# A sparse attention stage: its eight query blocks in a new order, top-k picks taken earlier, banded logits in mid-slot

## What is computed

```python
def swa_sink_attention(q, k, v, sinks, rel_table):   # banded: 8 heads, window 128
    ...
def block(args):                                     # sparse: once per 128 queries (block n)
    ql, iqb, iwb, n = args
    t = n * QB + jnp.arange(QB)
    dots = jnp.einsum('bqhd,bsd->bqhs', iqb, ik) * (IDX_DIM ** -0.5)
    score = jnp.einsum('bqh,bqhs->bqs', iwb, jax.nn.relu(dots))
    score = jnp.where(causal[None], score, NEG_INF)
    _, idx = lax.top_k(score, topk)                  # topk = 256
    ...
    logits = jnp.einsum('bqhc,bqkc->bhqk', ql, sel)  # plus bias of the distance
    p = jax.nn.softmax(logits, axis=-1)
    o_lat = jnp.einsum('bhqk,bqkc->bqhc', p, sel)
```

## Time and profile before

| what | us |
|---|---|
| median of 3 runs | 3803.22 |
| lowest and highest | 3801.25, 3818.11 |
| profiled execution, its own time | 3799.82 |
| its span | 3798.0 |
| TensorE, VectorE, ScalarE, GpSimd busy | 3341.8, 1476.6, 872.9, 745.3 |
| mean granted TensorE clock | 0.928 of full speed |

### The profile page before, as it was taken

One profiled execution on the slowest core, in us unless ns is written; L12 is line 12 of the kernel. 1 busy time (PEld: TensorE's weight loads), 2 busy tenths in 40 slices (PEclk: granted clock), 3 DMA queues, 4 the chain that ended last, 5 costly groups with the idle time before them and its releaser, 6 DMA issues.

```text
span 3798.0 us, 37215 instructions
## 1 busy us (share of the span) xinstructions
PE 3341.8 (88%) x14990; PEld 2463.6 (65%) x14990; DVE 1476.6 (39%) x2594; ACT 872.9 (23%) x1530; POOL 745.3 (20%) x322
## 2 busy tenths in 40 slices
PE   5996888887789878999999977999997589999998
PEld 2443344444677777788888854446877578888886
DVE  3013688998342135322222242302463722222225
ACT  2113333433312212111111122101341122112111
POOL 2000000000321103323323320001111433223223
PEclk9995788888889989999999988999998789999999
DMA  5100111111112101111111131010002202111112
GB/s 143 42 23 22 49 52 45 45 45 23 56 56 95 34 18 43 47 55 44 45 55 44 52 120 53 22 47 0 26 1 97 92 23 56 50 50 44 55 45 111
DMA packets 173178, 192.24 MB, mean 51 GB/s; under 512 B 24268, under 2 KB 137804, under 8 KB 172285
## 3 DMA queue, kind: packets, MB, share of 16 engines
q1 hardware_dynamic: 163696, 177.20, 14.8%
q10 hardware_dynamic: 9356, 13.31, 1.1%
HBM read 174.71 MB, written 15.78 MB: 50 GB/s over the span
## 4 chain that ended last, share of the span: by engine, by line
PE 60%; issue 16%; DVE 13%; POOL 6%; ACT 3%; DMA 1%; ACTq 1%; POOLq 0%; SPq 0%; DVEq 0%
PE psum L606 9%; PE psum L608 9%; PE psum L607 9%; PE psum L599 7%; PE psum L589 6%; POOL weights_parts L2150 3%; PE psum L971 3%; PE psum L709 2%; DVE x_cols L1596 2%; DVE rows L1594 2%; PE psum L703 2%; POOL region L2198 2%; DVE stats L1514 1%; PE psum L747 1%; PE psum L728 1%
## 5 line engine op out<-in xcount | busy, mean ns | idle before, releaser
L2150 POOL TENSOR_TENSOR weights_parts<-weights,weights_parts 128x2048 fp32r<-128x2048 f32 (+1 forms) x82 | 377.0, 4597 | 982.9 <-ACT weights_parts L1093 982.9
L606 PE MATMUL psum<-x_cols_parts,weights_parts 128*128 128x512 f32 x1344 | 525.0, 391 | 25.3 <-POOL weights_parts L2150 23.6
L608 PE MATMUL psum<-x_cols_parts,weights_parts 128*128 128x512 f32 x1344 | 524.3, 390 | 0.0
L608 PE MATMUL psum<-weights_parts,region_parts 128*128 128x512 f32 (+1 forms) x1120 | 410.0, 366 | 0.0
L606 PE MATMUL psum<-weights_parts,region_parts 128*128 128x512 f32 x864 | 337.2, 390 | 6.7 <-DVE region_parts L2104 5.8
L607 PE MATMUL psum<-weights_parts,region_parts 128*128 128x512 f32 x864 | 336.9, 390 | 0.0
L606 PEld LDWEIGHTS psum<-x_cols_parts,weights_parts 128*128 128x128 f32 x1344 | 253.4, 189 | 79.1 <-issue 24.6
L608 PEld LDWEIGHTS psum<-x_cols_parts,weights_parts 128*128 128x128 f32 x1344 | 253.2, 188 | 52.7
L607 PE MATMUL psum<-x_rows_parts,weights_parts 128*128 128x512 f32 x704 | 274.6, 390 | 0.0
L1093 ACT ACTIVATE weights_parts<-weights 128x2048 fp32r<-128x2048 f32 (+1 forms) x82 | 155.0, 1890 | 468.7 <-DMA region<-in_bup_h_dram 142.4
L606 PE MATMUL psum<-weights_parts,x_cols_parts 128*128 128x256 f32 x768 | 222.2, 289 | 27.8 <-POOL wide_parts L2176 11.7
(11 more groups left out here) (285 smaller groups left out, 5185.8 us busy)
## 6 DMA issues: line engine op xcount, KB each, us to landing
weights<-in_ada_w_dram SPq DMA_DIRECT2D x24, 1024.0 KB, 5.2
weights<-in_ffn_up_w_dram SPq DMA_DIRECT2D x44, 512.0 KB, 4.8
weights<-in_w_up_dram SPq DMA_DIRECT2D x16, 1024.0 KB, 5.1
weights<-in_w_down_dram SPq DMA_DIRECT2D x16, 1024.0 KB, 5.1
weights<-in_m_in_w_dram SPq DMA_DIRECT2D x7, 2048.0 KB, 9.1
weights<-in_ffn_down_w_dram SPq DMA_DIRECT2D x10, 1024.0 KB, 5.1
weights<-in_xa_wkv_dram SPq DMA_DIRECT2D x4, 2048.0 KB, 8.0
x_rows<-x_scratch SPq DMA_DIRECT2D x4, 2048.0 KB, 11.3
```

The lines of the kernel that those rows point to most:

```text
L606: pe.matmul(o, lhsT=a_hi, rhs=b_hi, start=(first and i == 0), stop=False)
L608: m = pe.matmul(o, lhsT=a_lo, rhs=b_hi, start=False, stop=(last and i == len(terms) - 1))
L2150: pool.tensor_tensor(WLO[buf][:, 0:width], WRAW[buf][:, 0:width], WHI[buf][:, 0:width], ALU.subtract).then_inc(s("w_lo"), 1)
```

## The change

- `ORDER = (1, 7, 6, 5, 4, 3, 2, 0)`: step n works on block `ORDER[n]`, and every width, slice and condition follows the block instead of the step. Steps 0 and 7 (blocks 1 and 0) need no pick.
- The picks of step 1 (block 7, 1024 columns) are spread over the 15 slots from (-1, 0) to (0, 6): two rounds in each of 13, three in the last two. The picks of later steps stay where they were relative to the step: four rounds in slot 7 of step m - 2, 28 in step m - 1.
- The index dots, Relu and sums of block 7 are done ahead of the loop, in PSUM banks 0 to 3, with two new semaphores, `ix0_l` and `ix0_e`; VectorE waits for `attn_in` behind them.
- VectorE's order in a slot: bias add, maximum, `index_sum`, `window_max`, the first half of the rounds, `window_scores`, reciprocal, second half, `window_sum`.
- The modulation pieces stay where they were: four in each of steps 1 to 6.

```diff
+ORDER = (1, 7, 6, 5, 4, 3, 2, 0)
+FIRST_ROUNDS = (2,) * 13 + (3, 3)
...
+def picking(n):
+
+    return 0 <= n < NT and ORDER[n] >= 2
+
+
+def pick_rounds(n, i):
+
+    g = NH * n + i + NH
+    if g < len(FIRST_ROUNDS):
+        a = sum(FIRST_ROUNDS[:g])
+        return 1, a, a + (FIRST_ROUNDS[g] + 1) // 2, a + FIRST_ROUNDS[g]
+    m, r = (n + 2, 0) if i == NH - 1 else (n + 1, 4 * i + 4)
+    return (m, r, r + 2, r + 4) if picking(m) else None
...
-    if k >= 2 and k < NT:
+    if k >= 2 and picking(k):
         jobs["ix0"] = ("ix", k, h, 0)
-        if (k + 1) * P > BW:
+        if (ORDER[k] + 1) * P > BW:
             jobs["ix1"] = ("ix", k, h, 1)
...
             pe.wait_ge(f_free, FT["memT"])
+            b = ORDER[1]
+            for h in range(NH):
+                hp = slice(DH * (h % 2), DH * (h % 2) + DH)
+                if h >= 2:
+                    pe.wait_ge(s("ix0_e"), h - 1)
+                for c in range(2):
+                    m = pe.matmul(PS[:, 2 * (h % 2) + c, 0:(b + 1) * P - BW * c if c else BW], lhsT=iqT[hp, h // 2, b * P:b * P + P],
+                                  rhs=ikT[hp, BW * c:min(BW * c + BW, (b + 1) * P)], start=True, stop=True)
+                m.then_inc(s("ix0_l"), 1)
...
-                if n >= 2:
-                    pe.wait_ge(s("picked"), n - 1)
...
+                L = (ORDER[n] + 1) * P
+                if picking(n):
+                    pe.wait_ge(s("picked"), n)
...
+            L = (ORDER[1] + 1) * P
+            for h in range(NH):
+                act.wait_ge(s("ix0_l"), h + 1)
+                if h >= 2:
+                    act.wait_ge(s("ix_s"), h - 1)
+                act.activation(RL[:, h % 2, 0:L], PSf[:, 1024 * (h % 2):1024 * (h % 2) + L], ACT.Relu,
+                               scale=DH ** -0.5).then_inc(s("ix0_e"), 1)
...
+            for h in range(NH):
+                index_sum(1, h)
+            dve.wait_ge(s("attn_in"), 16 * 7)
             mark(dve.tensor_tensor(bias[:, NH:2 * NH, :], bias[:, NH:2 * NH, :], over_last(far, 2 * P), ALU.subtract))
...
-                if i < 4 and m < NT:
+                if n >= 0 and picking(n + 2):
+                    index_sum(n + 2, i)
+                if i == 4 and 0 <= m < NT:
+                    window_max(m)
+                rounds = pick_rounds(n, i)
+                if rounds:
+                    pick(rounds[0], rounds[1], rounds[2])
+                if i < 4 and 0 <= m < NT:
                     window_scores(m, i)
-                if n >= 0 and 2 <= n + 2 < NT:
-                    index_sum(n + 2, i)
-                if i == 4 and m < NT:
-                    window_max(m)
-                if 2 <= m < NT and i < 7:
-                    pick(m, 4 * i + 4, 4 * i + 6)
-                if i == 7 and 2 <= n + 2 < NT:
-                    pick(n + 2, 0, 2)
                 if 0 <= g < NH * NT:
                     dve.wait_ge(s("d_e"), g + 1)
                     dve.reciprocal(dend[:, i:i + 1], dend[:, i:i + 1]).then_inc(s("d_r"), 1)
-                if 2 <= m < NT and i < 7:
-                    pick(m, 4 * i + 6, 4 * i + 8)
-                if i == 7 and 2 <= n + 2 < NT:
-                    pick(n + 2, 2, 4)
+                if rounds:
+                    pick(rounds[0], rounds[2], rounds[3])
...
+            causal(1)
             for m in range(NT):
-                if m >= 2:
-                    pool.wait_ge(s("ix_s"), NH * (m - 1))
...
+                if m >= 2 and picking(m):
+                    causal(m)
```

More of the change, by code:

```diff
@@ L82, in shared_jobs @@
         jobs["first"] = ("d_out", n - 1)
-    if i == 7 and m < NT:
+    if i == 7 and 0 <= m < NT:
         jobs["out"] = ("a_out", m, 0)
@@ L86, in shared_jobs @@
         jobs["out"] = ("a_out", n, i + 1)
-    if m < NT and i < 4:
+    if 0 <= m < NT and i < 4:
         jobs["banded"] = ("a_log", m, i)
-    if m < NT and i >= 6:
+    if 0 <= m < NT and i >= 6:
         jobs["turned"] = ("a_t", m, i - 6)
@@ L98, in shared_jobs @@
         jobs["ada"] = ("ada", 4 * (n - 1) + i // 2)
-    if m < NT and i == 6:
+    if 0 <= m < NT and i == 6:
         jobs["query0"], jobs["query1"] = ("query", m, 0), ("query", m, 1)
@@ L672, in window_logits @@
             def window_logits(m, e):
-                o, lo, q = shared(("a_log", m, e)), max(m - 1, 0), slice(m * P, m * P + P)
-                width, r = (m + 1 - lo) * P, e % 2
+                o, c0 = shared(("a_log", m, e)), ORDER[m]
+                lo, q = max(c0 - 1, 0), slice(c0 * P, c0 * P + P)
+                width, r = (c0 + 1 - lo) * P, e % 2
                 hp = slice(DH * r, DH * r + DH)
@@ L677, in window_logits @@
                     ins = pe.matmul(o[:, (c % 2) * 256 + 256 - width:(c % 2) * 256 + 256], lhsT=Q[hp, c, q],
[L678 removed]
+                                    rhs=kaT[hp, c // 2, lo * P:c0 * P + P], start=True, stop=True)
                 ins.then_inc(u_ready, 1)
@@ L712, in latent_query @@
             def latent_query(n, r):
-                o, q, hp = shared(("query", n, r)), slice(n * P, n * P + P), slice(DH * r, DH * r + DH)
+                o, q, hp = shared(("query", n, r)), slice(ORDER[n] * P, ORDER[n] * P + P), slice(DH * r, DH * r + DH)
                 for j in range(4):
@@ L722, in sparse_logits @@
                     pe.wait_ge(s("d_e"), g - 1)
-                if n >= 2:
-                    pe.wait_ge(s("picked"), n - 1)
-                for a in range(0, (n + 1) * P, BW):
-                    z = min((n + 1) * P, a + BW)
+                else:
+                    pe.wait_ge(s("ix0_e"), NH - 1 + g)
+                L = (ORDER[n] + 1) * P
+                if picking(n):
+                    pe.wait_ge(s("picked"), n)
+                for a in range(0, L, BW):
+                    z = min(L, a + BW)
                     o = PS[:, 2 * (g % 2) + a // BW, 0:z - a]
-                    ins = pe.matmul(o, lhsT=QL[:, g % NH, :], rhs=cT[:, a:z], start=True, stop=(n < 2))
-                    if n >= 2:
+                    ins = pe.matmul(o, lhsT=QL[:, g % NH, :], rhs=cT[:, a:z], start=True, stop=not picking(n))
+                    if picking(n):
                         ins = pe.matmul(o, lhsT=ident_h[:, :], rhs=MSK[:, n % 2, a:z], start=False, stop=True)
@@ L736, in sparse_transposes @@
                     pe.wait_ge(s("d_te"), g)
-                for kt in range(g // NH + 1):
+                for kt in range(ORDER[g // NH] + 1):
                     ins = pe.transpose(PS[:, 4 + kt // 4, (kt % 4) * P:(kt % 4) * P + P], LG[:, g % 2, kt * P:kt * P + P], ident[:, :])
@@ L1260, in _ @@
                     job(place)
-                if i == 4 and n + 1 < NT:
+                if i == 4 and 0 <= n + 1 < NT:
                     window_exp(n + 1)
@@ L1640, in _ @@
                 g, m = NH * n + i, n + 1
-                L = m * P
                 if 0 <= g < NH * NT:
+                    b = ORDER[n]
+                    L = (b + 1) * P
                     dve.wait_ge(s("d_l"), g + 1)
-                    near = slice(max(n - 1, 0) * P, L)
+                    near = slice(max(b - 1, 0) * P, L)
                     pair = PSf[:, 1024 * (g % 2):1024 * (g % 2) + L]
-                    dve.tensor_tensor(pair[:, near], pair[:, near], bias[:, NH + i, (P if n == 0 else 0):], ALU.add).then_inc(s("d_lb"), 1)
+                    dve.tensor_tensor(pair[:, near], pair[:, near], bias[:, NH + i, (P if b == 0 else 0):], ALU.add).then_inc(s("d_lb"), 1)
                 if 0 <= g < NH * NT:
```

69 lines of the change are left out of this document (37 added, 32 removed).

## The result

The changed kernel took **3748.1 us** (median of 4 runs, 3746.3 to 3751.5) against 3806.5 us before on the same chip: ratio 0.9844, 95% interval 0.9818 to 0.9869. (The forecast was worked out from three runs with a median of 3803.2; a fourth, of 3809.7, has moved the median since.) That is 58 us less, where I had forecast 31 (3772 for 3803.2); it lies inside the range of 3741 to 3806. The direction and most of the mechanism were right, the size was too small: the time lies nearer to rival E's 3741 than to my 3772.

A forecast was written before the change was run, and what follows sets the result against it. VectorE was taken to bound the attention stage's middle, latency chains its ends. Loop end 317 + 517 + 114 = 948 us against 976.3 (-28), drain -3: 3769, plus 3.4 for the median, 3772 us; range 3741 to 3806.

The forecast's parts named there:

- rival E: Late banded piece hides nearly all waits in steps 0 to 4, steps 5 and 6 mostly full clock: 3741; chance 0.17.
- part 1: Attention loop in the new order with early picks: VectorE's own time per step, sum 517 us with the lead-in.
- part 2: Index scores of block 7 ahead of the loop: it begins at 317 us instead of 303.9, bounds 313 and 326.5.
- part 3: Banded logits after two rounds: each step's first banded wait goes (1.8 us in one), the second stays as a rate.
- Rival D: Moving the banded piece does nothing, the bank being released later by as much: +14, 3786; chance 0.13.
- part 4: Modulation pieces: cost 0 where VectorE is the bound; in steps 5 and 6, 3.6 to 5.8 plus 0.9 us each.
- the waits: VectorE's waits that stay in steps 0 to 7 of the attention loop: sum 114 us.
- rival B: Light steps run at 1.2 GHz, giving 28 us back: 3800, no change to be told; chance 0.17.
- step 7: Last loop step, 128 columns: 25.5 us from 42.0 less eight times 2.1, of which 20 are waits.
- The drain: Behind the loop's end, one more ScalarE and TensorE round at 128 columns for 1024: -3 us, bounds 0 and -4.
- Step 0: First block of the loop (block 1): own time 71 us, waits 8 from two slots and the query slot at 0.50 clock.
- Rival C: TensorE becomes the bound of steps 0 to 5, up to 3.5 us per banded slot, 84 in all: 3856; chance 0.10.

The follow-up runs named there:

- experiment 3: The changed kernel with the order 1,7,2,3,4,5,6,0 in place of 1,7,6,5,4,3,2,0: 3792.4 us, ratio 0.9957.
- experiment 7: The changed kernel with block 7's 32 rounds as 1 in the first lead-in slot and 31 in the first seven slots of step 0: 3758.5 us.
- experiment 2: The kernel before, in its old order, with only the banded logits moved to mid-slot: 3813.3 us against 3809.7, ratio 1.0011.
- Experiment 5: The changed kernel with five modulation pieces in each of steps 1 to 4, four in step 5, none in step 6: 3754.2 us, ratio 0.9846.
- experiment 4: The changed kernel with each step's four modulation pieces in slots 3, 4, 5, 6 instead of 0, 2, 4, 6: 3770.3 us, ratio 0.9901.
- either control: The changed kernel itself, unaltered, run again twice beside other versions: first 3745.4 us (ratio 0.9829), second 3752.1 us (0.9844).
- experiment 6: The changed kernel with three dummy matmuls more at the end of each of the eight lead-in slots: 3749.6 us, ratio 0.9843.

## Why the prediction was right, and where it was short

**VectorE's own time (part 1): right.** Every step is within 1 us in the changed kernel. In experiment 3 the sum held too (514 us), while its forecast lengths missed by up to 10 us (step 4 with 106.3 for 96, 16.1 of it waits). Moving rounds from under a wide block without slack to places where VectorE stood is what pays: the lead-in (11 us by experiment 7), and the narrow blocks where nothing is left to pick (some 40 us by experiment 3).

**Index scores ahead of the loop (part 2): 5 us too dear.** I let two heads run at half clock and reckoned TensorE as the pace. Both held: the clock was 0.50 until 297.1 us and 1.00 behind it, and two heads took 3.1 us, 2.90 of them the eight instructions of L685, while VectorE's two sums took 2.67 and waited 0.42. Too dear was the price of a call, taken from another product (L589): two heads took 3.79 us at half clock, where I had 6.9, and 2.90 at full, where I had 3.4. The loop began 8.3 us later than before, for 10.2 us of work.

**Mid-slot banded logits (part 3): the reasoning held, the size not.** "The wait of the second is a rate of the bank" stands: 4.8, 4.3, 5.6, 3.3 and 2.6 us in steps 1 to 5, in each case the second piece; shorter waits came at later pieces as well (1.5 us at the fourth of step 1), and one of 1.5 us at the first of step 0. That the first wait simply goes did not hold in the old order (experiment 2): what the late release saves there is paid at the index sums. Rival D, that the move does nothing, is true of the old order and, by the traces, not of the new one.

**Modulation pieces (part 4)**: "cost 0 where VectorE is the bound" is at most true of the spacing they have, and no run left the four pieces out of steps 1 to 3 to show it. Experiment 5 shows a fifth piece in a step at 1.4 to 4.1 us, experiment 4 shows four in a row at some 20 us in all. In step 6 a piece cost 3.7 us, less than the 4.5 and more that I had.

**The terms that were mis-sized are the waits**, 114 us forecast, 94.2 measured: 29.6 less than forecast in the light steps 4 to 7, and 10.3 more in steps 0 to 3. In the light steps there were two errors. The first is rival B's subject: I put the light steps between the two clock levels. They ran at 0.92 to 0.99 in the profile above, 0.90 was the least in either control; for full clock the text had 51 us for step 6, and it took 48.6. The second is step 7, 15.8 us for 25.5. I subtracted 0.7 us for each of three operations from a slot of 4.8 us and got 2.7; the last five slots took 1.21 to 1.30 us each. The reason is that the slot was not made of those operations. Before, in such a slot of 1024 columns, from the timeline:

```profile
970.95 1.04 PE L738 MATMUL psum<-ident,region 128*128 128x128 f32 x8
...
971.83 1.95 PE L747 MATMUL psum<-region 128*128 128x128 f32 x16
971.98 1.22 DVE L1649 TENSOR_REDUCE rows<-psum 128x1 f32<-128x1024 f32 x1
972.03 1.02 ACT L1250 ACTIVATE region<-psum 128x1024 f32<-128x1024 f32 x1 [0.61 <-PE psum L738]
973.82 0.28 ACT L1258 ACTIVATE x_cols<-psum 128x128 f32<-128x128 f32 x1 [0.76 <-PE psum L747]
973.99 1.14 ACT L1235 ACTIVATE region<-region,rows 128x1024 f32<-128x1024 f32 x1
975.03 1.11 ACT L1243 ACTIVATE region<-psum,rows 128x1024 f32<-128x1024 f32 x1
```

ScalarE waited twice for TensorE, VectorE's reduction was over 1.8 us before exp began, and TensorE (logits, mask, transposes, values) shows no idle time at all from 957.1 to 971.5 us, three slots. As far as a busy time with modelled ends can tell, TensorE's own work made the 4.81 us of the slot, and my term left it out. After, at 128 columns:

```profile
919.51 0.37 ACT L1280 ACTIVATE region<-psum,rows 128x128 f32<-128x128 f32 x1
...
920.01 0.16 DVE L1705 RECIPROCAL rows<-rows 128x1 f32<-128x1 f32 x1 [0.53 <-ACT region L1280]
920.09 0.28 DVE L1690 TENSOR_TENSOR psum<-psum,x_cols 128x128 f32<-128x128 f32 x1
...
920.40 0.29 DVE L1693 TENSOR_REDUCE rows<-psum 128x1 f32<-128x128 f32 x1
...
920.73 0.37 ACT L1280 ACTIVATE region<-psum,rows 128x128 f32<-128x128 f32 x1
```

Here one exp follows the other over the reciprocal, the bias add and the reduction, 1.22 us, in which ScalarE's scaling (0.39) and its copy (0.27) find room. Over the eight slots this term was 9.7 us too dear. The drain after it gave back 4.9 us where I had put 3.

**Step 0 erred the other way**, 13.9 us of waits for 8 (17.7 in one control). I counted two slots and the query slot; five slots waited in the profile above, 4.8, 2.7, 2.7, 1.1 and 2.1 us. I had reckoned it at half clock throughout; it waited longer than that even where the clock was above it.

**Rival C (TensorE becomes the bound)** didn't come: TensorE was busy 89.4 of 105.4 us in step 1, and VectorE waited 6.8. **Rival E** came nearer to the time than the forecast did, and for half its reason: it was right about the clock of the light steps, and wrong in that the late banded piece would hide nearly all waits of steps 0 to 4. They were 38.6 us, for 32.5 in the forecast. That 3748 lies well inside the range is in part luck, as errors of both signs met: the waits above, 5 us at the start, and 8.5 us given back behind the stage.

**Of the signs named**, these came: the first MAX8 at 312.2 us, lead-in slots of 5.7 us without waits, step 1 at 105. These didn't: waits in second banded slots only, steps 5 and 6 near 60 us (57.2 and 48.6), the end near 948 (921.4). All of the last miss to the short side.

**After the stage some was given back.** The attention output was ready 59.9 us earlier (928.8 for 988.7), the span only 51.4 us shorter. Most of this lies in one later stage with short dependent jobs; one stretch of it took 33.5 us at a clock of 0.77 before and 38.4 at 0.62 in the profile above, with the same busy time of VectorE and ScalarE. It looks like chance and not the change: from the last weight split ahead of this stage to the first behind it the changed kernel took 700.3 us in the profile above, 693.4 in the first control and 699.6 in the second; the kernel before took 693.7. The traces of all experiments on the changed kernel lie within 1 us of 693.5 or of 700; experiment 2, in the old order, has 696.9.

The Trainium skill (TensorE: Matmul & The Clock Gate, Part 1) says that the slow clock is what an idle TensorE falls back to. The lead-in at 0.50 with TensorE busy 14.5 of 45.8 us agrees. What it would do to steps 5 and 6, the half clock of rival B, did not come: small jobs that keep TensorE busy 83 and 84% of the row held 0.97 and 0.99.

## What to carry to other kernels

Write the own time of the bounding engine as a sum per step from the rows of a trace: here it forecast that engine's own time under a new order to 1%. Then ask in which steps that engine stands, and put the steps that will stand for lack of work where everything else in them is narrow. Waits in a chain of small jobs don't go away by moving a job: here one job moved took its wait to another line, and three in a row made the waits longer. When a step loses its bound, look which engine has no idle time in it, TensorE included, and work out the next cycle from the rows, not from the wait that VectorE shows.

## What had not been expected

- The granted clock of two executions of one kernel differs in some steps (0.90 and 0.99 in step 6), and with it the step's time (52.4 and 48.6 us), while the steps around repeat to 0.2 us.
- TensorE busy 84% of step 0 had 0.58, busy 84% of step 6 had 0.99. The share of busy time in a row, whose ends are modelled, doesn't say which clock is granted. (The jobs of step 0 may be longer just because of the clock; this was not tested apart.)
- The mask of 128 columns on GpSimd took 2.20 us beside VectorE's bias subtraction, and 0.29 us in each of its six calls in the kernel before, so the cover of 2.28 us was used up: the mask began 0.23 us after the subtraction and ended 0.15 us behind it, and the first MAX8 waited 0.24 us. Why it was longer was not tested apart. The Trainium skill (SBUF — State Buffer, SBUF: two separate sides) says that VectorE, with two inputs from SBUF, and GpSimd share one pair of ports, and that the later one stands until the instruction of the earlier one is over; the trace agrees, with 309.87 + 2.20 = 312.07 against an end of 311.92 for L1680.
- With the clock at 0.75 for 0.50 the lead-in was no shorter: 47.1 us for 45.8, of which 1.2 are a wait for the first logits behind the dummy matmuls. In the lead-in the half clock cost nothing that shows; in step 0 it did (experiment 6).
